# Attention: the softmax scales of two heads made by one reciprocal and one product

## What is computed

```python
s = s + bias;  p_cmp = masked_softmax(s, dc >= 0)            # compressed branch
p = masked_softmax(s, mask_s);  o_slc = p @ vs                # four selected blocks of 64 keys
p = masked_softmax(s, mw);      o_win = p @ vw                # the last 256 keys
out = g0 * o_cmp + g1 * o_slc + g2 * o_win                    # gates, per head and token
```

## Time and profile before

| | |
|---|---|
| time, median of 3 executions | 4189.13 us (4184.47 to 4193.12) |
| span of the profiled execution | 4193.6 us, 63444 instructions |
| TensorE busy | 4014.7 us, 96% |
| VectorE busy | 2362.2 us, 56% |
| ScalarE busy | 1631.7 us, 39% |
| GpSimd busy | 421.9 us, 10% |
| the 32 units of attention | 1380 to 1905 us of the span |
| TensorE busy in those 525 us | 486.1 us |

### The profile page before, as it was taken

How to read it: one execution, slowest core, us unless ns; L and a number is a source line. 1 busy time by engine, 2 the same in 40 slices (tenths; PEclk the granted TensorE clock), 3 DMA queues, 4 the chain that set the end, 5 groups by cost and what they waited for, 6 DMA issues and landing times.

```text
span 4193.6 us, 63444 instructions
## 1 busy us (share of the span) xinstructions
PE 4014.7 (96%) x23002; PEld 3466.1 (83%) x23002; DVE 2362.2 (56%) x3482; ACT 1631.7 (39%) x2260; POOL 421.9 (10%) x439
## 2 busy tenths in 40 slices
PE   8999999998998799999699999999999999999998
PEld 6888888886787556557599999999999999999987
DVE  4444444445443676653455555555566666666678
ACT  3222222223342677673233332333334444444455
POOL 2000000000221233340100010010010100101010
PEclk8999999999999799999799999999999999999999
DMA  5222232223444311004333343344354555556566
GB/s 219 101 91 109 98 132 90 90 105 143 166 149 136 91 40 45 21 17 159 152 134 138 126 156 129 141 150 149 146 182 180 205 181 199 191 191 209 189 253 265
DMA packets 153671, 594.27 MB, mean 142 GB/s; under 512 B 26896, under 2 KB 54928, under 8 KB 113043
## 3 DMA queue, kind: packets, MB, share of 16 engines
q1 hardware_dynamic: 139076, 548.02, 36.2%
q0 software_dynamic: 10384, 35.14, 3.0%
q10 hardware_dynamic: 4080, 9.44, 0.6%
HBM read 535.76 MB, written 57.83 MB: 142 GB/s over the span
## 4 chain that ended last, share of the span: by engine, by line
PE 49%; DVE 1%; DMA 0%; issue 0%; ACT 0%; POOL 0%; DVEq 0%; POOLq 0%; SPq 0%; ACTq 0%
PE moe_ps L443 10%; PE moe_ps L445 10%; PE moe_ps L444 10%; PE moe_ps L485 5%; PE moe_ps L486 5%; PE moe_ps L487 5%; PE moe_ps L424 1%; PE moe_ps L452 0%; PE moe_ps L453 0%; PE moe_ps L456 0%; DMA moe_wd_raw<-in_moe_wd 0%; DVE moe_yacc L364 0%; DVE moe_ht_lo L323 0%; DMA moe_stage<-h_moe,moe_ids 0%; DVE moe_gu_lo L327 0%
## 5 line engine op out<-in xcount | busy, mean ns | idle before, releaser
L443 PE MATMUL moe_ps<-moe_ht_hi,moe_gu_hi 128*128 128x256 f32 (+4 forms) x3136 | 938.1, 299 | 1.6 <-DVE moe_ht_lo L323 1.6
L445 PE MATMUL moe_ps<-moe_ht_hi,moe_gu_lo 128*128 128x256 f32 (+4 forms) x3136 | 937.5, 299 | 0.0
L444 PE MATMUL moe_ps<-moe_ht_lo,moe_gu_hi 128*128 128x256 f32 (+4 forms) x3136 | 937.1, 299 | 0.0
L244 ACT CAST moe_gu_hi<-moe_gu_raw 128x2048 fp32r<-128x2048 f32 x226 | 430.9, 1907 | 522.0 <-PE moe_ps L445 490.4
L327 DVE TENSOR_TENSOR moe_gu_lo<-moe_gu_raw,moe_gu_hi 128x2048 fp32r<-128x2048 f32 x226 | 517.4, 2289 | 171.1 <-ACT moe_gu_hi L244 171.1
L443 PEld LDWEIGHTS moe_ps<-moe_ht_hi,moe_gu_hi 128*128 128x128 f32 x3136 | 597.0, 190 | 5.3 <-issue 1.8
L444 PEld LDWEIGHTS moe_ps<-moe_ht_lo,moe_gu_hi 128*128 128x128 f32 x3136 | 597.7, 191 | 3.5
L445 PEld LDWEIGHTS moe_ps<-moe_ht_hi,moe_gu_lo 128*128 128x128 f32 x3136 | 596.7, 190 | 0.0
L364 DVE SCALAR_TENSOR_TENSOR moe_yacc<-moe_ps,job_weights,moe_yacc 128x512 f32<-128x512 f32 x504 | 374.8, 750 | 326.7 <-PE moe_ps L487 326.7
L485 PE MATMUL moe_ps<-moe_wd_hi,moe_hid_hi 128*128 128x512 f32 x1008 | 396.3, 393 | 0.0
L486 PE MATMUL moe_ps<-moe_wd_lo,moe_hid_hi 128*128 128x512 f32 x1008 | 393.8, 391 | 0.0
(11 more groups left out here) (355 smaller groups left out, 6628.0 us busy)
## 6 DMA issues: line engine op xcount, KB each, us to landing
moe_gu_raw<-in_moe_wgu SPq DMA_DIRECT2D x228, 1024.0 KB, 4.8
moe_wd_raw<-in_moe_wd SPq DMA_DIRECT2D x112, 1024.0 KB, 6.7
first_gu<-in_ffn_wgu SPq DMA_DIRECT2D x58, 1024.0 KB, 4.8
ffn_wd_raw<-in_ffn_wd SPq DMA_DIRECT2D x28, 1024.0 KB, 6.8
kvq_lo<-qt SPq DMA_DIRECT2D x8, 1024.0 KB, 4.9
kt<-kt_rows SPq DMA_DIRECT2D x8, 1024.0 KB, 6.3
shared<-in_w_kvq SPq DMA_DIRECT2D x5, 1024.0 KB, 8.0
kvq_raw<-in_w_kvq SPq DMA_DIRECT2D x5, 1024.0 KB
```

What stands on the lines that cost most here:

```text
L244: act.copy(gu_hi[s][:, :, :, :].rearrange("p a k c -> p (a k c)"), gu_raw[r][:, :]).then_inc(s_gu_hi, 1)
L443: pe.matmul(out[:, 0:W], gu_hi[s][:, half, k, :], ht_hi[:, k, 0:W], start=(k == 0), stop=False)
L444: pe.matmul(out[:, 0:W], gu_hi[s][:, half, k, :], ht_lo[:, k, 0:W], start=False, stop=False)
L445: last = pe.matmul(out[:, 0:W], gu_lo[s][:, half, k, :], ht_hi[:, k, 0:W], start=False, stop=(k == KT - 1))
```

## The change

`scale_of` now takes four columns: one reciprocal of 128x4 and one product of 128x4 (with a strided view of the gates) make both scales of two heads, and it counts the semaphore up by two. VectorE calls it behind steps 1 and 5 in place of steps 1, 3, 5 and 7, with the two `scale_win` of the two heads behind it. The slots of the sums and scales are eight columns still, so each call also waits for both the even and the odd head of the unit before. `scale_even` moves on ScalarE from behind the exponentials of steps 3 and 7 to behind those of steps 6 (head 0) and 2 of the next unit (head 2).

```diff
-                        if b % 4 == 3:
-                            scale_even(k - 3)
+                        if b % 4 == 2 and k >= 6:
+                            scale_even(k - 6)
                         if u:
                             values_part(u - 1, b)
+            scale_even(8 * 4 * TILES - 4)
             for b in range(8):
                 values_part(4 * TILES - 1, b)
...
-                dve.wait_ge(s_exp, k + 2)
+                dve.wait_ge(s_exp, k + 4)
                 if k >= 8:
 
-                    dve.wait_ge(s_odd_scaled if b // 2 % 2 else s_even_scaled, (k - 8) // 4 + 1)
-                at, c = (4 * g + b // 2) * 3 + 1, slice(k % 8, k % 8 + 2)
+                    dve.wait_ge(s_even_scaled, (k - 8) // 4 + 1)
+                    dve.wait_ge(s_odd_scaled, (k - 8) // 4 + 1)
+                at, c = (4 * g + b // 2) * 3, slice(k % 8, k % 8 + 4)
                 chain.step(dve.reciprocal(sums[:, c], sums[:, c]))
-                dve.tensor_tensor(scale[:, c], gates[:, i, at:at + 2], sums[:, c], ALU.mult).then_inc(s_scale, 1)
+                dve.tensor_tensor(scale[:, c].rearrange("p (h b) -> p h b", b=2),
+                                  gates[:, i, at:at + 6].rearrange("p (h b) -> p h b", b=3)[:, :, 1:3],
+                                  sums[:, c].rearrange("p (h b) -> p h b", b=2), ALU.mult).then_inc(s_scale, 2)
...
-                        if b % 2 and 8 * u + b >= 3:
-                            scale_of(8 * u + b - 3)
+                        if b % 4 == 1 and 8 * u + b >= 5:
+                            scale_of(8 * u + b - 5)
+                            scale_win(8 * u + b - 4)
                             scale_win(8 * u + b - 2)
...
-            scale_of(8 * 4 * TILES - 2)
+            scale_of(8 * 4 * TILES - 4)
+            scale_win(8 * 4 * TILES - 3)
             scale_win(8 * 4 * TILES - 1)
```

## The result

The changed kernel takes **4224.39 us**, the median of four executions (4220.17 to 4230.07), against 4191.12 us for four of the kernel before on the same chip: ratio **1.0079**, 95% interval 1.0065 to 1.0093. That is slower by 33 us. The sign was as forecast and the time lies in the range (4204 to 4292), but the forecast was 72 us, over twice as much.

The account below looks back on a forecast made before the run. TensorE sets the pace, waiting for VectorE's step 2 bias. Terms 45 + 6 + 3 (step 5 and the end) + 11 + 7 = 72 us, added to 4189.1, gave 4261 us; 8-in-10 range 4204 to 4292.

Parts of the forecast that it names:

- What is removed: On VectorE, 64 pairs of reciprocal and product at 0.39 us, 25 us; counted at nothing from tile 2 on.
- Who gets in: Between VectorE's two back-to-back window scalings, the waiting GpSimd scaling gets in, so the second scaling waits.
- For how long: Behind step 1, the second window scaling is blocked for all of GpSimd's scaling, ending about 0.20 us behind it.
- The main term: Step 2 bias late by GpSimd's scaling time less 0.2 us at each step 1, units 8 to 31: 45 us.
- ScalarE: Moved scale_even in step 2 delays the first key tile's copy, so TensorE's turning waits: 11 us.
- Tiles 0 and 1: Units 1 to 7 lose time to blocking at steps 1 and 5, less removed pairs: 6 us.
- Step 5: Same blocking there, mostly covered by VectorE's wait ahead of step 6: 2 us, for tiles 2 to 4.
- Clock: Longer TensorE gaps in g = 2 units add clock falls to 1.2 GHz in units 14 and 26: 7 us.
- Rival (a): Second window scaling not blocked; step 2 bias late 7 us, scale_even costs 9 more: 4205 us, chance 0.14.
- (b): More clock falls: seven of ten new TensorE gaps add 28 us and more, 4295 us and above; chance 0.05.
- (c): Faster: removed pairs lie on the path ahead of step 0 and in tiles 0 and 1; 4180 us, chance 0.05.
- (d): No change: delays at step 1 are eaten by the gap ahead of step 0, 0.5 us a unit; chance 0.04.

Follow-up runs that it names:

- odd_waits: The changed kernel, but GpSimd's scaling waits until VectorE has done both window scalings; 4204.87 us, ratio 1.0033 to the kernel before.
- split: The changed kernel with its placement, but each head again has its own two-column reciprocal and product; 4218.52 us, ratio 1.0068 to the kernel before.
- probe: The kernel before with 14 extra VectorE scalings of 64 columns to a spare tile behind step 1 in six units; profiled 4228.0 us.
- the square: Changed kernel; without collision; without ScalarE's move; without either: 307.3, 298.4, 304.1, 294.8 us over 17 units whose clock stayed at 1.00.
- late: The changed kernel with the first group behind step 2 (1 in the last three units) and scale_even back at steps 3 and 7; 4202.28 us, ratio 1.0021.
- cmp_later: The kernel before with VectorE's three pieces for the next tile, and GpSimd's scale_cmp, later in the g = 2 units; 4180.18 us, ratio 0.9963.
- wins: The kernel before with both window scalings behind steps 1 and 5, reciprocals and products still four; 4204.60 us, ratio 1.0031.
- nudge_four: The changed kernel with four one-column GpSimd writes to a spare tile between its wait and its scaling; 4228.25 us, 0.80% above before.

## Why the prediction was right in sign and wrong in size

**The bound.** Right. TensorE waits for the bias of step 2, and what VectorE does between steps 1 and 2 comes back in the unit's length: a pair shorter by 0.75 us made unit 27 shorter by 0.76 (odd_waits).

**What is removed.** Right in that it gains nothing: split puts those 64 pairs back, and in the 15 units where its pair of step 1 is free it is as long as odd_waits within 0.13 us. But the 25 us are too many. A common pair takes 0.48 us from the reciprocal to the scaling and not 0.39, so VectorE saves 128 x 0.39 - 64 x 0.48 = 19 us, and the four-column forms, counted at nothing, put 0.09 us ahead of each bias of step 2, 2 us over 24 units.

**Who gets in.** Right. The prediction took, from the first stage, that the one that waits gets in between two. In after 61 of 64 pairs were interrupted so; in the other three GpSimd did not start just behind the first scaling.

**For how long: the step that failed.** "So one blocks the other for a whole operation" was read from a row at the end of an operation: 0.57 us for a scaling that came 0.37 us ahead of GpSimd's end. That row shows that VectorE is blocked at the end and says nothing on the middle. The others that took 0.73 us lay under GpSimd's bias (L1552), an operation of 0.61 us and not its scaling. The probe shows the middle of the scaling open. The Trainium skill says the same as the prediction ("SBUF — State Buffer", section "Who interferes with whom"): whoever issues first has the pair of ports for the whole instruction, and the other blocks fully. By that rule the pair of unit 27 would have lasted to 0.2 us behind GpSimd's end, 3.0 us; it took 1.50. The measurement decides: for GpSimd's scaling by a column of factors the block is two pieces, not one.

With the pairs as measured (0.84 us at 256 columns, then 1.08, 1.18, 1.29, 1.40, 1.50, and 1.61 at 1024) the bias is late by the pair less 0.46 or 0.47. The main term becomes 0.37 + 4 x (0.61 + 0.71 + 0.82 + 0.93 + 1.03) + 3 x 1.14 - 2.85 = **17 us in place of 45**. This one term is 28 of the 39 us by which the forecast of 72 missed the measured 33. It is borne out by the stretch from the reciprocal of step 1 to the bias of step 2: over the 17 units it takes 30.7 us after, 14.0 more than before, and those units are 17.5 us longer, of which 3.6 are ScalarE's.

**ScalarE.** Mechanism right, size too large. Its list by unit adds up to 10.3 us, put down as 11. The waits view agrees with it (16.4 - 5.5 = 10.9), but taking the move back gives 0.22 us in unit 27 and 0.85 in unit 29, where the prediction had 0.6 and 1.9 (the 1.9 with the late bias in it). Over the seven of the 17 units that had a price, 5.1 were predicted and 2.2 measured, with the collision and without. So a wait that grows in the view is not time lost one for one. Unit 25 (g = 1), which the prediction did not list, lost 0.76 or 1.01.

**Tiles 0 and 1.** 6 us predicted; units 0 to 7 took 78.8 us before and 84.0 after, 5.2 more. Unit 3 alone differs by 2.0, with a clock of 0.79 in place of 1.00, so this agreement is partly luck.

**Step 5.** Taken at 2 us, on VectorE's pause ahead of step 6. Right that it is next to nothing: nine interrupted pairs there did not make split's units longer. The 16 clean units from tile 2 on say the same. Step 1 explains them by itself: the second scaling's excess there sums to 3 x (0.33 + 0.43 + 0.54 + 0.65 + 0.75) + 0.86 = 9.0 us, and over the same 16 units the square gives 8.7 and 9.1. The units outside the sum were not tested so.

**Clock.** Wrong as a term. The gaps grew as predicted and a little less, to 3.98 and 4.09 us:

```profile
1703.41 1.65 PE L1816 MATMUL att_s<-kt,kvq_lo 128*128 128x512 f32 x4 [3.98 <-DVE att_neg_max L1759]
...
1790.50 1.40 PE L1816 MATMUL att_s<-kt,kvq_lo 128*128 128x512 f32 x4 [4.09 <-DVE att_neg_max L1759]
```

But the mean clock of unit 26 fell only from 1.00 to 0.93 and that of 30 too, unit 14 stayed (0.90 and 0.91), and units 10 and 18 rose (0.72 to 0.80, 0.77 to 0.92). Already before, unit 26 had shown 1.00 behind the same gap as unit 22; to count two more falls was to forecast the toss of a coin. Nor is it so that the clock fell only behind gaps of 2.7 us and more, as the prediction read it: the fall in unit 30 came 1.3 us behind a gap of 1.58 us, and in late all five g = 2 units from 10 to 26 fell, behind gaps of 2.02 to 2.20 us. Many new falls in other units did not come.

**Rival (a)**, second scaling not blocked, 4205 us, would have needed pairs of 0.75. That kernel was made, by making GpSimd wait: odd_waits, 4204.87. The price of the place, 7 us there for the units from 8 on, is 5.0 us over 16 of those 24 and unit 5; the match of the two times to 0.1 us is luck, as its ScalarE term of 9 us is too large. Rivals (b), (c) and (d) are out by the time alone: 4224 is far from 4295, and it is clearly slower.

## What to carry to other kernels

Joining two small operations on an engine with room saves nothing; look at what it bunches. Here some 19 us of VectorE's time were saved and 33 us lost, since two scalings that share a resource with GpSimd came to stand back to back, in the one place where TensorE waits next, with GpSimd released at the same moment. Price such a block by the piece of the other operation that overlaps it, measured with small operations laid through it, and not by a row that happens to fall at its end. And before polishing a step, look what else stands ahead of the same wait: moving other VectorE work, 2.9 us of it out of this very place, gave 15 us (cmp_later, 0.37%) with no operation removed.

## What the runs showed of the hardware

- GpSimd's scaling blocks VectorE's in two pieces. At 1024 columns, 3.09 us: until some 1.14 us behind its start, then again over the last 0.7 to 0.9 us (an estimate from the probe's times); in between four scalings of 64 columns took their free 0.73 us.
- The other way round GpSimd waits for VectorE's first scaling: 2.75 us against 2.53 at 896 columns, 0.22 us. VectorE's selected bias takes no longer beside GpSimd: 0.81 us in unit 27 after, and 0.82 us in unit 27 of the probe, where GpSimd stood still.
- Started 0.05 to 0.10 us behind the first of two scalings, GpSimd always got in between them; started 0.17 to 0.19 us behind, it did in 18 of 64 cases of one kernel, 15 of 64 of another and 53 of 61 of a third (wins, split, nudge_four).
- Joined to four columns, reciprocal and product took 0.17 and 0.16 us as with two, but the product started 0.28 us behind the reciprocal in place of 0.19.
- TensorE's clock fell to 0.50, 1.2 GHz, behind gaps of 2.7 to 2.9 us in some executions and units and not in others, and it did so behind 2.02 to 2.20 us in late and 1.58 us in unit 30 after. With the gaps of the g = 2 units taken out it was 1.00, 2.4 GHz, in all of them from unit 14 on; in unit 10, where a gap of 2.09 us was left, the mean was 0.90.
